# mLSTM cell: heads written as a pipeline, side work spread among the input panels, one root per head

## The reference, cut to what matters

```python
p = h @ w_in                                  # 4 * 768 + 8 + 256 columns
qk = silu(causal_conv(p[..., :2 * W], conv_w))
v = p[..., 2 * W:3 * W]
o = p[..., 3 * W:4 * W]
gates = p[..., 4 * W:4 * W + 8] + gate_bias   # i and f rows, one of each per head
q_mem = p[..., 4 * W + 8:]
cell = mlstm_chunkwise(q, k, v, i, f)         # num / max(|den|, exp(-m))
cell = rms_norm_2(cell, h_gain)               # per head, over its 192 features
h_a = sigmoid(o) * cell
h_m = memory_cross_attention(q_mem, ...)      # normalises q_mem per head first
return concatenate([h_a, h_m]) @ w_out
```

## Time and profile before

| what | us |
|---|---|
| median of 3 runs (4008.15 to 4011.63) | 4010.6 |
| the profiled execution | 4012.29 |
| its span in the trace | 4010.5 |
| PE busy | 3676.9 (92%) |
| DVE busy | 2169.8 (54%) |
| POOL busy | 1919.2 (48%) |
| ACT busy | 1500.0 (37%) |

### The profile page before, as it was taken

How to read it: one execution, slowest core, us unless ns; L and a number is a source line. 1 busy time by engine, 2 the same in 40 slices (tenths; PEclk the granted TensorE clock), 3 DMA queues, 4 the chain that set the end, 5 groups by cost and what they waited for, 6 DMA issues and landing times. The chain is left out here.

```text
span 4010.5 us, 50702 instructions
## 1 busy us (share of the span) xinstructions
PE 3676.9 (92%) x17222; PEld 3075.7 (77%) x17222; DVE 2169.8 (54%) x3437; ACT 1500.0 (37%) x2610; POOL 1919.2 (48%) x1474
## 2 busy tenths in 40 slices
PE   7889998988999999999979867999979998589999
PEld 6468998978999999888868425888758886357887
DVE  7772997867999766633235246333333322654330
ACT  3433555743333333543213214433234422343332
POOL 4523774446888786555414103444434543014444
PEclk9989999989999999999989768999989999689999
DMA  4022554569999898333323101333223335102332
GB/s 130 21 63 76 165 173 150 212 256 356 400 405 402 314 357 298 104 95 94 95 88 99 32 0 42 99 92 92 90 63 96 98 91 101 43 22 89 94 93 90
DMA packets 172656, 569.72 MB, mean 142 GB/s; under 512 B 15458, under 2 KB 58594, under 8 KB 155013
## 3 DMA queue, kind: packets, MB, share of 16 engines
q1 hardware_dynamic: 152244, 427.68, 32.8%
q0 software_dynamic: 20304, 140.78, 9.4%
HBM read 518.33 MB, written 50.07 MB: 142 GB/s over the span
## 5 line engine op out<-in xcount | busy, mean ns | idle before, releaser
L271 POOL TENSOR_TENSOR weight_low<-weight_ring,weight_high 128x512 fp32r<-128x512 f32 x1264 | 1725.2, 1387 | 1812.5 <-ACT weight_high L243 1367.0
L285 PE MATMUL banks<-normed_high,weight_high 128*128 128x512 f32 (+1 forms) x2528 | 951.4, 376 | 54.3 <-ACT weight_high L243 29.0
L286 PE MATMUL banks<-normed_low,weight_high 128*128 128x512 f32 (+1 forms) x2528 | 942.5, 373 | 0.0
L243 ACT ACTIVATE weight_high<-weight_ring 128x512 fp32r<-128x512 f32 x632 | 398.8, 631 | 1389.2 <-PE banks L292 1306.4
L285 PEld LDWEIGHTS banks<-normed_high,weight_high 128*128 128x128 f32 x2528 | 485.0, 192 | 125.6 <-issue 44.1
L292 PE MATMUL banks<-normed_high,weight_low 128*128 128x512 f32 (+1 forms) x2528 | 572.6, 368 | 6.0 <-POOL weight_low L271 5.7
L286 PEld LDWEIGHTS banks<-normed_low,weight_high 128*128 128x128 f32 x2528 | 484.6, 192 | 62.1 <-issue 2.6
L292 PEld LDWEIGHTS banks<-normed_high,weight_low 128*128 128x128 f32 x2528 | 461.3, 188 | 67.9 <-POOL weight_low L271 9.2
L245 ACT ACTIVATE weight_high<-weight_ring 128x512 fp32r<-128x512 f32 (+1 forms) x632 | 389.9, 617 | 92.4 <-PE banks L292 82.4
L2031 DVE TENSOR_TENSOR square<-square,banks 128x512 f32<-128x512 f32 x88 | 60.6, 689 | 416.4 <-PE banks L292 414.9
L285 PE MATMUL banks<-parked_high,weight_high 128*128 128x384 f32 x768 | 262.5, 342 | 15.6 <-ACT weight_high L243 10.0
(11 more groups left out here) (369 smaller groups left out, 5726.5 us busy)
## 6 DMA issues: line engine op xcount, KB each, us to landing
weight_ring<-in_experts SPq DMA_DIRECT2D x256, 512.0 KB, 5.8
weight_ring<-in_ffn_gate SPq DMA_DIRECT2D x88, 512.0 KB, 3.6
weight_ring<-in_ffn_up SPq DMA_DIRECT2D x88, 512.0 KB, 3.6
weight_ring<-in_ffn_down SPq DMA_DIRECT2D x64, 512.0 KB, 3.5
expert_gates<-spread_space SPq DMA_DIRECT2D x6, 4096.0 KB, 12.3
parked_space<-expert_gates SPq DMA_DIRECT2D x24, 768.0 KB, 8.9
parked_space<-parked_activations SPq DMA_DIRECT2D x24, 768.0 KB, 10.9
weight_ring<-in_a_w_in SPq DMA_DIRECT2D x28, 512.0 KB, 3.6
```

Of the source, the lines that this page charges most:

```text
L243: m.nc.scalar.activation(m.w_hi[:, s % PARTS, 0:HALF], m.ring[:, s, 0:HALF], ACT.Copy).then_inc(m.half_high, 1)
L271: m.nc.gpsimd.tensor_tensor(m.w_lo[:, s % PARTS, at], m.ring[:, s, at], m.w_hi[:, s % PARTS, at].bitcast(FP), ALU.subtract).then_inc(done, 1)
L285: m.nc.tensor.matmul(out, w_hi, hi(c), start=(first and c == 0), stop=False)
L286: m.nc.tensor.matmul(out, w_hi, lo(c), start=False, stop=False)
```

## The change

The computation of the cell is written in a new order, in three parts.

- **Among the panels.** The panel order is new (`CELL_ORDER`): the two gate rows first, then the two chunks of the memory query, then six groups of two q/k panels and one value panel, then the six gates. The PE loop is written out for all 28 panels. Between panels PE makes the sums for the norm of the memory query (after panel 7), the 4-column transposes (8), the spread of the four m rows (10) and the four guard rows (15), and the transposes of the values (18 to 21, 23, 25). ACT and DVE do their parts of these in the same loops. The negated m rows and the guard rows of all four heads are kept in the space `rows`.
- **Heads as a pipeline.** The buffers for the weights and the masked diagonal exist twice, the sums alternate between banks 4, 5 and 6, 7. PE makes the scores of head h + 1 before the values of head h. The mask is added by POOL. The values are laid out with 64 columns of ones beside each half piece, so that the product with the half piece gives the row sums in the other 64 partitions, and the separate product with ones is gone.
- **One root.** The quotient and its norm are folded: with n the numerator and d the larger of |den| and the guard, n/d normalised is n / sqrt(mean(n²) + eps·d²). ACT squares both numerator pieces out of PSUM (the den squares with them), DVE takes the maximum with the squared guard, PE adds both up with a product of ones per piece, and there is one root and one reciprocal per head. The output gate is multiplied in before.

The block of the norm and the block of `head_rms` are gone from the cell; attention follows on the heads.

```diff
+CELL_ORDER = [("row", 0), ("row", 1), ("qm", 0), ("qm", 1)] + \
+             [o for k in range(ML_CHUNKS) for o in (("qk", 2 * k), ("qk", 2 * k + 1), ("v", k))] + \
+             [("gate", c) for c in range(ML_CHUNKS)]
...
+def turn_value(m, pe, act, values_t, values, c, turned, read):
+    bank = m.bank[4 + c % 4]
...
+    if c in (1, 4):
+        at = value_columns(0 if c == 1 else 2)[1]
+        m.nc.scalar.activation(values[:, :, at:at + HD], src[:, :, 0:HD], ACT.Copy)
+        ins = m.nc.scalar.activation(values[:, :, at + P:at + P + HD], src[:, :, HD:P], ACT.Copy)
...
             scale.sums(pe)
-            panel_products(m, pe, IN)
-            pe.wait_ge(evac, QK + C)
-            turn_values(m, pe, None, values_t, values, C, v_turned, v_read)
+            for j in range(IN):
...
+                if j == 7:
+                    for k in range(2):
+                        pe.wait_ge(q_squared.sem, q_squared.base + k + 1)
+                        nc.tensor.matmul(m.bank[4 + k][:, :], m.const[:, BLOCK:BLOCK + P], sq[:, k, :], ...
+                if j == 8:
+                    pe.wait_ge(row_steps, SUMS)
...
+                if j == M_AT:
+                    pe.wait_ge(q_rooted.sem, q_rooted.base + 2)
+                    pe.wait_ge(cols, 2)
+                    for h in range(R):
+                        nc.tensor.matmul(m.bank[4 + h][:, :], sel(h), m_row, start=True, stop=True).then_inc(spread, 1)
+                if j == G_AT:
+                    pe.wait_ge(row_steps, BOUND)
...
+                if j == 7:
+                    act.wait_ge(row_steps, SUMS)
+                    nc.scalar.activation(g_row, g_row, ACT.Exp, scale=-2.0).then_inc(row_steps, 1)
...
+                if j == 6:
+                    dve.wait_ge(row_steps, LN)
+                    order.step(dve, vec.tensor_scalar(f_row, f_row, 0.0, None, ALU.min))
...
+                if j in (12, 15):
+                    k = (12, 15).index(j)
+                    dve.wait_ge(q_rooted.sem, q_rooted.base + k + 1)
+                    order.step(dve, vec.reciprocal(qm_root[:, k, :], qm_root[:, k, :]))
...
         @block.tensor
-            for h in range(ML_HEADS):
-                if h:
-                    pe.wait_ge(celled, h)
-                nc.tensor.matmul(NUM[0][:, :], sel(h), m_row, start=True, stop=True).then_inc(spread, 1)
-                nc.tensor.matmul(GUARD[:, :], sel(h), g_row, start=True, stop=True)
...
-                    ins = nc.tensor.matmul(DEN[:, sb * P:T], m.const[:, ONES:ONES + P], w[:, sb, 0:T - sb * P],
-                                           start=(sb == 0), stop=(sb == TT - 1))
+            score(0)
+            for h in range(H):
+                if h + 1 < H:
+                    score(h + 1)
+                if h:
+                    norm_sum(h - 1)
+                values_of(h)
+            norm_sum(H - 1)
...
+        @block.gpsimd
+            for h in range(H):
...
+                nc.gpsimd.tensor_tensor(sets[h % 2][1], neg_m[h].rearrange("p (s t) -> p s t", s=TT),
+                                        mask.unsqueeze(1).to_broadcast([P, TT, P]), ALU.add).then_inc(negated, 1)
...
+            def norm_root(h):
+                act.wait_ge(total, h + 1)
...
+                nc.scalar.activation(root[h % 2], m.bank[3][:, :], ACT.Sqrt, scale=1.0 / ML_HD).then_inc(rooted, 1)
...
+            def close(h):
+                dve.wait_ge(squared, 2 * h + 2)
+                vec.scalar_tensor_tensor(out=sq[rest, 1, :], in0=sq[rest, 1, :], scalar=3 * EPS, in1=guard[h][rest, :],
+                                         op0=ALU.mult, op1=ALU.max).then_inc(bounded, 1)
...
+            weigh(0)
+            for h in range(H):
+                if h:
+                    close(h - 1)
+                if h + 1 < H:
+                    weigh(h + 1)
+                if h:
+                    finish(h - 1)
+            close(H - 1)
+            finish(H - 1)
...
-    sq = space.cut(C * T, C, T)
-    squared = m.sem("ml_squared")
...
-    head_rms(m, lambda c: qm[:, c, :], lambda c: qm[:, c, :], lambda c: m.v("mem_q", 0), 2, T, space)
```

More of the change, by code:

```diff
@@ L2475, in _, with bias_row, shape @@
             order = m.scalar_order
+            def bias_row(k, row):
+                act.wait_ge(evac.sem, evac.base + k + 1)
+                at_v = VEC[("gate_i", "gate_f")[k]]
+                order.step(act, nc.scalar.activation(row, row, ACT.Identity, bias=m.vec[0:R, at_v:at_v + 1]))
+            def shape(j):
+                kind, c = CELL_ORDER[j]
+                if kind == "gate":
+                    act.wait_ge(evac.sem, evac.base + j + 1)
+                    nc.scalar.activation(out_gate[:, c, :], out_gate[:, c, :], ACT.Sigmoid)
             scale.root(act)
@@ new lines, in _ @@
+                if j == 3:
+                    bias_row(0, i_row)
+                    bias_row(1, f_row)
+                    order.step(act, nc.scalar.activation(l_row, f_row, ACT.Abs))
+                if j == 4:
+                    order.step(act, nc.scalar.activation(l_row, l_row, ACT.Exp, scale=-1.0))
+                    nc.scalar.activation(l_row, l_row, ACT.Ln, bias=1.0).then_inc(row_steps, 1)
+                if j == 5:
+                    for k in range(2):
+                        act.wait_ge(evac.sem, evac.base + place["qm", k] + 1)
+                        nc.scalar.activation(sq[:, k, :], qm[:, k, :], ACT.Square).then_inc(q_squared.sem, 1)
@@ new lines, in _ @@
+                if j in (G_AT + 1, G_AT + 2):
+                    act.wait_ge(spread, 2 * R)
+                    for h in ((0, 1), (2, 3))[j - G_AT - 1]:
+                        nc.scalar.activation(guard[h], m.bank[4 + h][:, :], ACT.Copy, scale=3 * EPS)\
+                            .then_inc(spread_read, 1)
+                if j - 1 in TURN_AT:
+                    c = TURN_AT.index(j - 1)
+                    if c == 0:
+                        act.wait_ge(q_scaled.sem, q_scaled.base + 2)
+                    turn_value(m, None, act, values_t, values, c, v_turned, v_read)
@@ L2557, in _, with score @@
         def _(pe):
[L2558 to L2567 removed]
+            def score(h):
@@ L2587, in _, with exponents @@
         @block.scalar
         def _(act):
-            act.wait_ge(cols, 1)
-            m.scalar_order.step(act, nc.scalar.activation(ccol.rearrange("p s h -> p (s h)"), COLS[:, 0:TT * R], ACT.Copy))
-            act.sem_inc(cols, 1)
-            for h in range(ML_HEADS):
+            def exponents(h):
+                w, diag = sets[h % 2]
                 act.wait_ge(negated, h + 1)
@@ L2606, in _, with weigh @@
             order, vec = m.vector_order, nc.vector
-            for h in range(ML_HEADS):
-                dve.wait_ge(spread, h + 1)
-                order.step(dve, vec.tensor_scalar(neg_m, NUM[0][:, :], -1.0, None, ALU.mult))
-                vec.tensor_tensor(diag, neg_m.rearrange("p (s t) -> p s t", s=TT),
-                                  mask.unsqueeze(1).to_broadcast([P, TT, P]), ALU.add).then_inc(negated, 1)
+            def weigh(h):
+                w = sets[h % 2][0]
                 for sb in range(TT):
@@ new lines, in finish @@
+            def finish(h):
+                dve.wait_ge(rooted, h + 1)
+                order.step(dve, vec.reciprocal(root[h % 2], root[h % 2]))
+                dve.wait_ge(gated, h + 1)
+                for i, (c, at) in enumerate(pieces(h)):
+                    ins = vec.tensor_tensor(cell[at, c, :], cell[at, c, :], root[h % 2][at, :], ALU.mult)
+                ins.then_inc(scaled, 1)
+            weigh(0)
+            for h in range(H):
+                if h:
+                    close(h - 1)
+                if h + 1 < H:
+                    weigh(h + 1)
+                if h:
+                    finish(h - 1)
```

339 lines of the change are left out of this document (203 added, 136 removed).

## The result

| | us |
|---|---|
| kernel before, median of 4 runs (4008.15 to 4011.63) | 4009.84 |
| changed kernel, median of 4 runs (3906.51 to 3915.67) | 3914.31 |
| ratio, with its 95% interval | 0.9755 [0.9742, 0.9769] |
| the profiled execution, and its span | 3915.23, 3913.5 |

The forecast was 3907, range 3896 to 3946. The profiled executions differ by 97.1 us. Nothing behind the attention's start moved (1584.3 us of span before and now), and the block begins 2.1 us later in its span (2086.84, now 2088.97), in work that is the same. Between these points the stretch is 339.4 us before and 240.2 now, 99.1 less.

What follows compares the result with a forecast made beforehand. Behind the last panel a chain of PE, ACT and DVE, no engine full, was taken to bound 183.8 us; the new stretch, 16 + 1.7 + 62 + 0.3 = 80, saves 104, so 4012.29 - 104 = 3908, less 1.7 surplus 3907 us; range 3896 to 3946.

Steps and rivals of the forecast that it cites:

- Among the panels, 16 us: Side work of PE between input panels: 13.0 us of products plus 3 for insertion points and a clock dip.
- 3 for insertions and a dip: Among the panels: 3 us taken for ten insertion points and a clock dip in the 4-row spreads, without a row.
- bound of 8 on top of 13.0: Among the panels: insertion points and clock dip cost between 0 and 8 us beyond the 13.0 of products.
- ACT's wait after panel 6: Among the panels: ACT waits about 5 us for the gate rows, at no cost; up to 5 us once if uncovered.
- The heads, 62 and 0.3: From barrier to attention: 15.5 + 24.4 + 21.3 = 61.2, with 0.8 for collisions 62 us, and 0.3 for the barrier to attention.
- open end: End of the heads, from the values of head 2 through head 3's scaling, no scores left as cover: 21.3 us.
- the rule on the shared port: In the heads: by the skill's GpSimd/VectorE port lock, POOL's masks could delay DVE, adding 5 us at most.
- Low clock when the heads begin: Rival: PE's 2 us idle at the barrier lowers the clock for scores 0 and 1; +13 us, 3920; chance 0.17.
- Scores cannot keep the clock: Rival: the clock falls in the heads' scores; 3937, chance 0.15, or low throughout 3961, chance 0.03.
- Late hand-over: Rival: DVE's `close` or `finish` delays a weighing PE awaits, a pause in three heads; 18 us, 3925; chance 0.09.
- chain after all: Rival: bank waits keep the heads a chain, only norm, query and gate rows saved; 47 less, 3964; chance 0.03.
- panels slower: Rival: written-out loop with 10 more waits makes ACT's splits late in each panel; 4021 at 4.2 us per panel; chance 0.02.

Runs made afterwards that it cites:

- no barrier: Kernel with late table wait, single spreads and scores 0 right behind the panels, now without the all-engine barrier before the heads: median 3903.33 us, ratio 0.9733.
- the doubled products: Changed kernel with the first two of the eight products of the values made twice in each head: 3931.64 us.

## Why the prediction was right, point by point

- **The base: 183.8 us behind the last panel are a chain.** Right: what the stretch lost, the kernel lost, but for 2.1 us that the block began later.
- **Among the panels, 16 us.** Mis-sized: 20.4. Of the 13.0 for products: the query sums cost 1.77 for 1.92, small transposes 0.57 for 0.5, the six lots of value transposes 0.47 each, 2.8 for 2.9, the two lots of spreads 5.46 and 7.06 for 3.84 each. The spreads were thus 4.84 over, and the dips explain it: 10.2 us at 1.2 GHz instead of 2.4 are 5.1 lost. The "3 for insertions and a dip" covered only part. The start cost 2.73 us more than before, 1.9 of it the wait for `side`. The prediction never named that wait, which stands in the changed kernel ahead of the first panel, and so put it at nothing. The bound of 8 on top of 13.0 held.
- **ACT's wait after panel 6 hidden.** Right: PE is busy 162.80 of 162.80 us. The loop written out cost nothing, as the earlier trace rows had it.
- **After the last panel 1.7.** 2.0 (2264.88 to 2266.89).
- **The heads, 62 and 0.3.** 62.3, but that it fits so well is luck, since terms balance. The parts that run at the full clock were 15.54 for 15.5 and 23.98 for 24.4, the latter with values starts 11.9 apart, predicted 12.2. In each of them scores cost 5.6 to 5.8 and values 4.3 to 4.4 where I took 5.15 for both: the average of the two was right, the assumption of equal price wrong. The open end was 22.8 for 21.3, and there the clock dips in the two norm sums cost 3.0; without them (no barrier) it is 19.8, 1.5 under the prediction.
- **DVE fits under PE.** Right: no wait of PE for DVE up to values 2, and the doubled products stayed on the path. The 0.8 for collisions was not needed. Products of two SBUF tensors took 0.69, and no mask on POOL ran beside one, so the heads do not test the rule on the shared port. The trace of the kernel before does, and the prediction missed it. The 1.044 us was no price but a mean: of the six products of L2666 four took 0.68 to 0.69 us, and the two that began while POOL made low parts (L450, 2406.66 to 2409.93) took 1.77 and 1.76. So such an overlap costs DVE 1.1 us a product.

```profile
L2666 DVE TENSOR_TENSOR mlstm_space<-mlstm_space x6: 677/689/1767, 2405.2 to 2410.4; 128x512 f32<-128x512 f32 x6
```

- **The rivals.** "Low clock when the heads begin" did not decide the profiled run, but is real: two of seven profiles with that pause, at 8 to 10 us, not 13. "Scores cannot keep the clock" is wrong: 1.00 over 11.2 us. Its evidence was right, though, and meant something else: they did not *raise* it. "Late hand-over", "chain after all" and "panels slower" did not occur. The last one's 4021 is also 4 us short of its own working (28 x 4.2 us on top of 3907).
- **Sum.** New stretch 84.7 for 80.0, all but 0.3 of the difference in the panels. The median, 3914.31, is 7.3 over the forecast 3907: these 4.7, the 2.1 us by which the block begins later in unchanged work, and 0.5 that is within the differences between runs.

What stays open: how often the clock is low after the barrier, how much of the run-to-run spread that makes beside the 9.6 us elsewhere in the program, and whether the rows or the change between them keep it low in the scores.

## What to carry to other kernels

Read a chain's clock as part of its price: a pause costs itself and the slow products behind it, so closing pauses pays twice (here 5.4 to 6.5 us and 5 more a head), and the first pause to close is the one ahead of work in which the clock did not rise again. Put few-row products one by one among full ones, not in lots, but expect little: 2.3 us in the panels for eight of them. A barrier waits for every engine's last instruction: moving work ahead of it on one engine delays what the others begin behind it, so move the others' first steps too, or drop the barrier. Look up what each new wait waits for, above all one at the start of a list. And a gain of a few us in one profile says little where runs of one kernel spread over 20 and unchanged work alone over 9.6. Ask of each forecast that came true where the time was gained.

## What the runs showed of the hardware that I had not expected

- With products with 4 rows, four in a row, the clock fell while PE was never idle (0.58 and 0.54 in the windows behind them); one at a time it stayed (1.00 over 161 us).
- Scores of 128 and 64 rows held 1.2 GHz for 21 us of full activity, and kept 2.4 GHz when they began at it. With 128 rows in all of them the clock was back after 3.1 us.
- A set of 16 score instructions that alternate between 128 and 64 rows took 5.78 us, with 128 rows throughout 4.32, at the same clock.
- A DVE product of two SBUF tensors (128x512) took 0.69 us alone and 1.77 where POOL's low parts ran beside it, in the kernel before.
